# Past attention of a two-layer hybrid trunk: queries stationary in fp32, score rows turned back per four units, values fetched through a table of row numbers

## The reference, cut to what matters

```python
# layer 0, FoX, 8 heads of 64: 8 sequences x 4096 past keys, in pages of 128
k_all = concat([cache_fox_k[page_table], k]);  v_all = concat([cache_fox_v[page_table], v])
s  = einsum('bqhd,bkhd->bhqk', q, k_all) * ATTN_SCALE + cum_q - cum_k      # forgetting bias
y  = einsum('bhqk,bkhd->bqhd', softmax(where(k_idx <= pos, s, -inf)), v_all)

# layer 1, dilated, 16 heads of 64: 8 sequences x 2048 past keys, of which 1280 are within reach
for w, d in ((128, 1), (512, 4), (2048, 16)):
    idx = q_idx - d * arange(w // d + 1)          # gathered keys of one group
    m, den, o = softmax parts over k_all[idx], v_all[idx]
y  = sum(den * exp(m - max m) * o) / sum(den * exp(m - max m))
```

## Time and profile before

| | us |
|---|---|
| median of 3 runs (2656.17 to 2666.19) | 2663.16 |
| the profiled execution | 2651.5 |
| its span, first to last instruction | 2649.8 |
| PE busy | 2269.1 (86%) |
| DVE busy | 1437.8 (54%) |
| ACT busy | 872.1 (33%) |
| POOL busy | 344.8 (13%) |
| past attention of `fox`, first K transpose to last value | 244 to 616 |
| past attention of `dilated` | 1831 to 2140 |

### The profile page before, as it was taken

One profiled execution on the slowest core, in us unless ns is written; L12 is line 12 of the kernel. 1 busy time (PEld: TensorE's weight loads), 2 busy tenths in 40 slices (PEclk: granted clock), 3 DMA queues, 4 the chain that ended last, 5 costly groups with the idle time before them and its releaser, 6 DMA issues. The chain is left out here.

```text
span 2649.8 us, 64653 instructions
## 1 busy us (share of the span) xinstructions
PE 2269.1 (86%) x26373; PEld 1768.7 (67%) x26373; DVE 1437.8 (54%) x2313; ACT 872.1 (33%) x1577; POOL 344.8 (13%) x555
## 2 busy tenths in 40 slices
PE   6898888887977996889999979997867776999998
PEld 3566777776635883667777757654766655777776
DVE  2446887874563537664522265466666656453323
ACT  2335444441231212333322131155333323333222
POOL 1003233430000000101100000023111110111000
PEclk8889999998977986899999989998788788999999
DMA  7324899994274001123323324443999931332331
GB/s 249 105 84 135 317 366 381 368 387 143 85 258 120 4 3 34 48 72 91 92 80 88 88 74 141 136 151 84 274 265 287 281 94 40 89 94 80 88 88 60
DMA packets 308578, 392.58 MB, mean 148 GB/s; under 512 B 25616, under 2 KB 226650, under 8 KB 308308
## 3 DMA queue, kind: packets, MB, share of 16 engines
q1 hardware_dynamic: 276580, 282.15, 34.6%
q0 software_dynamic: 31728, 106.59, 12.4%
HBM read 377.98 MB, written 10.70 MB: 147 GB/s over the span
## 5 line engine op out<-in xcount | busy, mean ns | idle before, releaser
L820 PE MATMUL bank<-yT,WH 128*128 128x288 f16 x3200 | 533.4, 290 | 46.1 <-DVE yT L674 34.6
L820 PEld LDWEIGHTS bank<-yT,WH 128*128 128x128 f16 x3200 | 314.8, 99 | 145.2 <-issue 48.6
L884 DVE SCALAR_TENSOR_TENSOR WL<-wring,WH 128x1024 f16<-128x1024 f32 x194 | 255.3, 1320 | 259.5 <-ACT WH L864 259.4
L1367 DVE TENSOR_TENSOR KL<-bank,KH 128x512 f16<-128x512 f32 x416 | 280.6, 688 | 168.7 <-ACT KH L1347 160.4
L1347 ACT CAST KH<-bank 128x512 f16<-128x512 f32 x416 | 242.2, 584 | 353.3 <-PE bank L1265 352.1
L820 PE MATMUL bank<-uT,WH 128*128 128x288 f16 x2048 | 337.9, 288 | 10.7 <-DVE WL L884 10.7
L820 PE MATMUL bank<-yT,WL 128*128 128x288 f16 x1600 | 331.8, 290 | 0.0
L864 ACT ACTIVATE WH<-wring 128x1024 f16<-128x1024 f32 x194 | 203.5, 1054 | 268.4 <-PE bank L820 221.0
L820 PEld LDWEIGHTS bank<-uT,WH 128*128 128x128 f16 x2048 | 201.5, 98 | 63.2 <-DVE WL L884 11.3
L820 PE MATMUL bank<-uT,WL 128*128 128x288 f16 x1024 | 210.7, 288 | 0.0
L820 PE MATMUL bank<-hT,WH 128*128 128x288 f16 x960 | 162.2, 293 | 31.8 <-DVE hT L711 21.4
(11 more groups left out here) (452 smaller groups left out, 3975.2 us busy)
## 6 DMA issues: line engine op xcount, KB each, us to landing
wring<-in_ada_w SPq DMA_DIRECT2D x96, 512.0 KB, 4.5
vslot<-in_cache_fox_v POOLq DMA_DIRECT2D x182, 256.0 KB, 5.5
vTd<-in_state_dil_k SPq DMA_DIRECT2D x80, 512.0 KB, 12.8
vslot<-in_state_dil_v POOLq DMA_DIRECT2D x78, 512.0 KB, 12.7
yT<-in_cache_fox_k SPq DMA_DIRECT2D x128, 256.0 KB, 5.5
krows<-in_cache_fox_k SPq DMA_DIRECT2D x128, 256.0 KB, 5.4
wring<-in_mlp_up SPq DMA_DIRECT2D x64, 512.0 KB, 4.0
wring<-in_mlp_down SPq DMA_DIRECT2D x64, 512.0 KB, 3.9
```

The costliest lines, as they stand in the source:

```text
L820: last = nc.tensor.matmul(bank[b + h][:, 0:HALF], w[s % 2][:, c, :], x[:, s % parts * KC + c, h * HALF:(h + 1) * HALF], start=(s % parts = ...
L884: nc.vector.scalar_tensor_tensor(WL[s % 2][:, :, :], w[:, :, :], WSCALE, WH[s % 2][:, :, :], ALU.mult, ALU.subtract).then_inc(w_free, 1)
L1367: nc.vector.tensor_tensor(KL[i][:, :], turned[n % NT][:, :], KH[i][:, :], ALU.subtract).then_inc(lo_out, 1)
```

## The change

The change does the following.

1. Keys are no longer split in two f16 parts. The turned bank is copied once in fp32 (`KT`), by ACT for three units of four and by DVE for each fourth (`by_dve`: n % 4 == 1). `KH` and `KL` go. Two PSUM banks hold turned keys where there were three; the third (`backed`) takes scores turned back.
2. `products`: the queries are the weights (128x32, fp32) and the keys move (128 columns). Head pair j writes partitions 32j to 32j+31, by a tile position. Q has 32 columns a pair: 16 for an even unit and 16 for an odd one, zero elsewhere, so that an even and an odd unit add into the same 128 columns. Scores come out with queries on partitions and cached rows along the columns.
3. New steps per group of four units: ACT copies 256 columns of scores to SBUF (`take_scores`, `SQ`), PE turns them back (`turn_back`, two 128x128 fp32 transposes), DVE adds the bias in two instructions of 128 columns where there was one of 256. The DVE and softmax steps stand one slot later (`BACK = LAG + 1`), and `LEAD` goes from 2 to 3 and from 0 to 1.
4. Q: a memset of 2048 columns and 16 scalings in both layers, without the two f16 parts.
5. V of `fox` on POOL: one indirect DMA of 128 rows of 4 KB a tile, with row numbers from a table `vrow_of` in SBUF. The table is made in `load_and_turn`: a broadcast load of the page table by POOL, and four small DVE instructions between the fifth and the sixth copy of the conditioning. SP's own V loads keep the two page DMAs.
6. The loads of `lora` and `g2` (512 KB) leave POOL's list in `load_and_turn` and come at the start of `rwkv` on SP; their first reader waits for them.

The instruction order of PE in the middle of `fox` shows points 1 to 3. Before, for two units in a row: the transposes of one unit (`yT` and `krows` are K slots), then the products of the unit two before.

The diff, cut to its core:

```diff
@@ -565,8 +569,17 @@
                     copy_group(3)
                     page_rest(1)
                     copy_group(4)
+                    dve.wait_ge(pa_in, 16)
+                    nc.vector.tensor_copy(pt_f[:, :], pt_all[:, :]).then_inc(pf_ok, 1)
+                    dve.wait_ge(pf_ok, 1)
+                    nc.vector.tensor_tensor(pt_odd[:, :], pt_f[:, 1::2], pt_f[:, 0::2], ALU.subtract).then_inc(pf_ok, 1)
+                    dve.wait_ge(pf_ok, 2)
+                    nc.vector.scalar_tensor_tensor(pt_odd[:, :], pt_odd[:, :], C["place"][:, 0:1], pt_f[:, 0::2], ALU.mult, ALU.add).then_inc(pf_ok, 1)
+                    dve.wait_ge(pf_ok, 3)
+                    nc.vector.tensor_scalar(vrow_of[:, :], pt_odd[:, :], float(PAGE // 2), C["place"][:, 1:2], ALU.mult, ALU.add).then_inc(pf_ok, 1)
...
         LAG = 2
         VLAG = nu + LEAD
-        turned = [bank[i] for i in (0, 1, 6)]
+        BACK = LAG + 1
+        turned = [bank[0], bank[1]]
         scored = [bank[2], bank[3]]
+        backed = bank[6]
         mixed = [bank[5], bank[7]]
         NT = len(turned)
         with ExitStack() as sc:
...
-            KH = [sb(sc, f"KH{i}", [P, 512], F16) for i in range(NB)]
-            KL = [sb(sc, f"KL{i}", [P, 512], F16) for i in range(NB)]
+            KT = [sb(sc, f"KT{i}", [P, 512]) for i in range(NB)]
+            SQ = [sb(sc, f"SQ{i}", [P, 256]) for i in range(2)]
...
+
+            by_dve = lambda n: n % NB == 1
+
+            def wait_copied(eng, n):
+
+                if by_dve(n):
+                    eng.wait_ge(kt_d, n // NB + 1)
+                else:
+                    eng.wait_ge(kt_a, n // NB * (NB - 1) + max(n % NB, 1))
 
...
                         last.then_inc(kt_ok, 1)
 
                     def products(n):
-                        v, i, g = n // nu * E + n % E, n % NB, n // SG
-                        pe.wait_ge(lo_out, n + 1)
+                        i, g, pair, even = n % NB, n // SG, n % SG // 2, n % 2 == 0
+                        wait_copied(pe, n)
                         if n % SG == 0 and g >= 2:
-                            pe.wait_ge(sc_out, g - 1)
+                            pe.wait_ge(sq_out, g - 1)
                         for j in range(4):
-                            o = scored[g % 2][:, (n % SG) * 64 + 16 * j:(n % SG) * 64 + 16 * j + 16]
-                            jc = slice(j * P, (j + 1) * P)
-                            nc.tensor.matmul(o, KH[i][:, jc], QH[:, v, j, :], start=True, stop=False)
-                            nc.tensor.matmul(o, KH[i][:, jc], QL[:, v, j, :], start=False, stop=False)
-                            last = nc.tensor.matmul(o, KL[i][:, jc], QH[:, v, j, :], start=False, stop=True)
+                            last = nc.tensor.matmul(scored[g % 2][32 * j:32 * j + 32, pair * P:(pair + 1) * P], Q[:, n // nu * 2 + n % 2, j, :],
+                                                    KT[i][:, j * P:(j + 1) * P], start=even, stop=not even, tile_position=(0, 32 * j),
+                                                    skip_group_check=True)
                         last.then_inc(sc_ok, 1)
+
+                    def turn_back(g):
+                        pe.wait_ge(sq_out, g + 1)
+                        if g:
+                            pe.wait_ge(sc_out, 2 * g)
+                        for pair in range(2):
+                            cols = slice(pair * P, (pair + 1) * P)
+                            last = nc.tensor.transpose(backed[:, cols], SQ[g % 2][:, cols], ident)
+                        last.then_inc(bk_ok, 1)
...
+                        n = i - BACK
+                        if 0 <= n < N and n % SG == SG - 1:
+                            turn_back(n // SG)
...
                 def _(act):
-                    def high(n):
+                    def take_turned(n):
                         i = n % NB
                         act.wait_ge(kt_ok, n + 1)
                         if n >= NB:
                             act.wait_ge(sc_ok, n - NB + 1)
-                        nc.scalar.copy(KH[i][:, :], turned[n % NT][:, :]).then_inc(hi_out, 1)
+                        nc.scalar.copy(KT[i][:, :], turned[n % NT][:, :]).then_inc(kt_a, 1)
+
+                    def take_scores(g):
+                        act.wait_ge(sc_ok, (g + 1) * SG)
+                        if g >= 2:
+                            act.wait_ge(bk_ok, g - 1)
+                        nc.scalar.copy(SQ[g % 2][:, :], scored[g % 2][:, 0:256]).then_inc(sq_out, 1)
...
                 @block.vector
                 def _(dve):
-                    def low(n):
+                    def take_turned(n):
                         i = n % NB
-                        dve.wait_ge(hi_out, n + 1)
-                        nc.vector.tensor_tensor(KL[i][:, :], turned[n % NT][:, :], KH[i][:, :], ALU.subtract).then_inc(lo_out, 1)
+                        dve.wait_ge(kt_ok, n + 1)
+                        if n >= NB:
+                            dve.wait_ge(sc_ok, n - NB + 1)
+                        nc.vector.tensor_copy(KT[i][:, :], turned[n % NT][:, :]).then_inc(kt_d, 1)
 
                     def half(g):
                         s, gs = divmod(g, NG)
                         if gs == 0 and s >= 2:
                             dve.wait_ge(o_ok, s - 1)
-                        dve.wait_ge(sc_ok, (g + 1) * SG)
+                        dve.wait_ge(bk_ok, g + 1)
                         u0 = gs * SG
-                        view = lambda x: x.rearrange("p (t h q) -> p t h q", t=SG // E, q=8)
-                        nc.vector.tensor_tensor(view(ST[s % 2][:, u0:u0 + SG, :].rearrange("p t c -> p (t c)")), view(scored[g % 2][:, 0:64 * SG]),
-                                                bias_of(s, u0 // E, SG // E), ALU.add).then_inc(sc_out, 1)
+                        for b in range(2):
+                            nc.vector.tensor_tensor(ST[s % 2][:, u0 + b:u0 + SG:2, :].rearrange("p a (h q) -> p a h q", q=8),
+                                                    backed[:, 0:256].rearrange("p (a h b q) -> p a h b q", a=2, b=2, q=8)[:, :, :, b, :],
+                                                    bias_of(s, u0, b), ALU.add).then_inc(sc_out, 1)
                         if gs % 2 == 1 or gs == NG - 1:
                             p = gs // 2
-                            dve.wait_ge(sc_out, g + 1)
...
 
 
-        dst, high, rest = Q
-        zero, qb_ok = sem("zero"), sem("qb_ok")
+        zero, q_ok = sem("zero"), sem("q_ok")
 
         def on_dve(dve):
-            n = 0
-            nc.vector.memset(dst[:, :, :, :], 0.0).then_inc(zero, 1)
+            nc.vector.memset(Q[:, :, :, :], 0.0).then_inc(zero, 1)
             dve.wait_ge(zero, 1)
-            for half in range(halves):
+            for b in range(2):
                 for j in range(4):
                     for hp in range(2):
                         r = slice(64 * hp, 64 * hp + 64)
-                        n += 1
-                        nc.vector.tensor_scalar(dst[r, half::halves, j, 8 * hp:8 * hp + 8], dec(src[r, 4 * half + j, NPR:TOK]), SCALE, None,
-                                                ALU.mult).then_inc(qb_ok, 1)
-            dve.wait_ge(qb_ok, n)
-            nc.vector.tensor_copy(high[:, :, :, :], dst[:, :, :, :]).then_inc(qb_ok, 1)
-            dve.wait_ge(qb_ok, n + 1)
-            nc.vector.tensor_tensor(rest[:, :, :, :], dst[:, :, :, :], high[:, :, :, :], ALU.subtract).then_inc(qb_ok, 1)
-            dve.wait_ge(qb_ok, n + 2)
+                        at = 16 * hp + 8 * b
+                        nc.vector.tensor_scalar(Q[r, b::2, j, at:at + 8], dec(src[r, (4 * b if halves == 2 else 0) + j, NPR:TOK]), SCALE, None,
+                                                ALU.mult).then_inc(q_ok, 1)
+            dve.wait_ge(q_ok, 16)
         return on_dve
...
+            load_k, load_v_pages = load_page("cache_fox_k"), load_page("cache_fox_v")
+            v_rows = I["cache_fox_v"][0].rearrange("n (p e) h d -> (n p) (e h d)", e=2)
+
+            def load_v(eng, n, dst, done):
+
+                if eng is nc.sync:
+                    load_v_pages(eng, n, dst, done)
+                else:
+                    nc.gpsimd.indirect_dma_start(dst[:, :], None, v_rows, bass.IndirectOffsetOnAxis(ap=vrow_of[:, n:n + 1], axis=0),
+                                                 bounds_check=320 * PAGE // 2 - 1, oob_is_err=False).then_inc(done, 16)
 
             def first_reads(sp):
...
                 sp.dma_start(rc[:, :], I["cst_rwkv"]).then_inc(rc_in, 16)
+                sp.dma_start(lora[0:64, :], I["rw_w2"][0]).then_inc(lora_in, 16)
+                sp.dma_start(lora[64:128, :], I["rw_a2"][0]).then_inc(lora_in, 16)
+                sp.dma_start(g2[:, :], I["rw_g2"][0]).then_inc(lora_in, 16)
```

73 lines of the change are left out of this document (42 added, 31 removed).

## The result

The changed kernel takes 2670.76 us (median of 17 runs, 2653.53 to 2680.66), the kernel before beside it 2658.04 (17 runs): ratio 1.0038, interval 1.0022 to 1.0054. It is slower by some 10 us, within the 0.5% that was called no change. A second comparison, on the chip of the first four experiments, gave 1.0026. The forecast was 2665.5, as a sum of +2.3 us on the kernel before. The time lies 5 us from it and the sign is right, but the difference is four to six times the sum. The inside came out otherwise as well: a term that was put at nothing is +22 us, and the stage that was called bound by the transfers was not at their limit.

A forecast was written before the change was run, and what follows sets the result against it. Transfers were taken to bound `fox` and `dilated`. The terms 0 + 1.7 + 1.2 + 1.0 - 1.1 - 0.5 = +2.3 us, on the 2663.16 median, gave 2665.5 us; whole range 2645 to 2700, the forecast's own 2653 to 2677.

The forecast's parts named there:

- The steady part of `fox`, "no change": `fox` past attention, 294 to 594 us: transfers set the pace at 1.39 us a unit, 377 GB/s; change 0.
- The prediction's own sign of being wrong: Changed profile of `fox`: GB/s off 377 by over 2% would show the forecast wrong.
- TensorE's unit: Past attention: PE's unit goes from 1.06 to 1.18 us, 1.26 at the granted clock, under 1.39 in `fox`.
- the rival of 1.92 us a unit: Both pasts: 32-column products don't overlap and PE becomes the bound, 136 us in `fox`, 74 in `dilated`, 2873; chance 0.06.
- The table, "nearest: no change": V loads in `fox`: between 15 us saved and 53 lost, no change taken; POOL is not waited for in the steady part.
- The drains: Ends of the two pasts, forecast with one filling slot each: `fox` +1.7 us net, `dilated` +1.2.
- the softmax part of the step (+0.9): Drain of each past: last softmax waits for `take_scores`, `turn_back` and two more handovers, some 0.9 us each.
- the table's landings: `fox` drain: last values wait for V, table loads land later than page loads; 0 to 3.3 us, 1.5 taken.
- Small edits: Query steps 3.4 to 5.3 us in `fox`, +1.0 taken; `dilated` 1.1 less; moved `lora` and `g2` loads 0.5 less.
- The filling part: `fox`, 260 to 290 us: SP's unchanged list sets K's pace, 1.24 us a unit at 224 GB/s; one slot loses 0.3 us.
- `dilated`, "no change": `dilated` past attention: PE's unit of 1.44 us stays under the transfers' 1.88, near 279 GB/s; change 0.
- DVE and ACT: Past attention: both far from binding, ACT under 0.6 us a unit; what they are relieved of is not on the path.

The follow-up runs named there:

- the first four experiments: Changed kernel again, ratio 1.0026 to the kernel before; changed kernel with V by page, 0.9965; kernel before with the table alone, 0.9956; changed kernel in pairs of slots, 0.9928.
- the pairs with the later softmax: Pairs of slots with the table, in `fox` softmax steps three slots later and values two, against the kernel before: 2619.17 us, ratio 0.9834.
- by page: Changed kernel with V of `fox` loaded by page DMAs on POOL again, all else as changed, against the kernel before: 2650.6 us, ratio 0.9965.
- the run with five extra matmuls: Kernel before with the table and five unused fp16 matmuls of 128 columns in each unit of `fox`: 2662.35 us, ratio 1.0002.
- the old form with the table: Kernel before with V of `fox` fetched through the table and nothing else changed: 2647.01 us, ratio 0.9956.
- The pairs: Changed kernel with TensorE's list written two units at a time, halving changes of tile shape: 2640.77 us, ratio 0.9928; with V by page 2656.67 us, 1.0003.

## Why the prediction came out as it did

**The steady part of `fox`, "no change": this step failed.** It is +22 us in the changed kernel (22.6 and 22.0). The reasoning was that the transfers set the pace at 1.39 us a unit, because the DMA share was 1.00, so that 1.18 or even 1.26 of TensorE was covered. The transfers' pace is 332.9/256 = 1.30 us a unit or less, at 395 GB/s. The prediction's own sign of being wrong was a rate off 377 GB/s by over 2%; 349 is off by 7%. A share of 1.00 was no ceiling: packets of 4 KB took 170 ns in the mean before and 166 in the pairs with the later softmax, and the sixteen engines count as busy in both. The 397 of the start stood in the earlier trace rows and was used only as a bound for the table. The Trainium skill has the rule that would have asked the question ("Perfetto Trace Analysis", Roofline): a single busy core is bounded by its sixteen DMA engines at about 435 GB/s, not by its 358 share. The runs agree so far as 395 GB/s held over 300 us.

**TensorE's unit: right in kind, too small.** Forecast 1.18, measured 1.28 without waits. Transposes and products with their changes of shape were put at 0.90 and took 0.94. The turn-back was put at 0.24 for a group and took 0.37, and the values at 0.88 and took 1.00: both have a change of shape of their own, which I had given only to the products. The products did overlap, 0.36 with the changes, so the rival of 1.92 us a unit fell.

**Cover was read as all or nothing.** 1.28 against the 350.8/256 = 1.37 of the kernel before leaves 7% of room, and I treated this as full cover. Data arrive unevenly, and TensorE had been making up for each late tile by groups down to 4.35 us. With its shortest group at 5.13 us it waits 30.9 us for K with the table, and loses; by page it waits 10.4 us at the same pace, and `fox` is only 3 us over the kernel before. So the reasoning missed that the two edits meet in K's transfers. How much of the loss is TensorE's pace is open, since the run with five extra matmuls lost its time otherwise. What these runs support is a question and not a rule: how far the shortest time of the covered engine lies below the bound, and not only its mean.

**The table, "nearest: no change".** Right for its rows: 377 GB/s in the old form. Wrong in that I looked only for a price of the rows. I had written that POOL is not waited for; what it does with its time when it is faster was left out. It now waits for the values and asks for two tiles 1.3 us apart, and in the changed kernel K's tiles come later. In the old form it does the same and nothing is lost, so the strokes alone are not the cause. Asking for the second tile some 0.3 us later took 9 us of the 19 back; the rest stays open.

**The drains.** Forecast +1.7 and +1.2. `fox` was 2.4 shorter, and 2.1 shorter in the old form with the table, 0.9 longer with pages alone. So the softmax part of the step (+0.9) would fit, while the table's landings, for which I took 1.5 us from the two loads of the start, cost nothing: the table gives back 2 to 3 us there. In `dilated`, from the last key transpose to the end of the stage, TensorE took 17.7 us for 18.1, so the +0.9 does not show.

**Small edits.** The query steps were as worked out:

```profile
141.87 1.76 DVE L1506 MEMSET Q<- 128x2048 f32 x1 [0.38 <-DVE qkT L921]
143.66 3.50 DVE L1513 TENSOR_SCALAR Q<-qkT 64x64 f32<-64x64 f32 x16
147.20 1.23 DVE L897 SCALAR_TENSOR_TENSOR WL<-wring,WH 128x1024 f16<-128x1024 f32 x1
```

That is 5.3 us for 3.4. Their part in the time can't be seen: the first K transpose came at 242.3 to 248.2 us in the ten executions with them and at 244.0 to 246.9 in the four without. The filling part moved 214 GB/s for 224, as steady as was forecast.

**`dilated`, "no change".** This held: 1.28 against 1.88 is room enough, and 289.4 to 300.2 is no different from the old form's 292.6 to 295.6. The pairs took it to 275.4 to 278.1 in three of four executions, so TensorE's pace had a part in it all the same.

**DVE and ACT.** That their relief (241 to 139 us of DVE in 300) would bring nothing was right for the changed kernel. It was half the truth: the order of VectorE's list costs TensorE time at each start of a sequence, in the kernel before as well, and I had read no waits by place in the sequence.

That the whole came near 2665.5 is luck. The kernel before is 2658.04 us in 17 runs, 5 us below the three that the forecast stood on, and the medians differ by 12.7 us for the 2.3 of the sum. Against the 22 us of `fox` stand two things that were not forecast: the shorter drain, and time elsewhere. Ten executions with the table took 1197.9 to 1211.5 between the pasts, four with pages 1209.8 to 1214.2, with nearly the same instructions; the granted clock falls at another point of that part. Whether the table causes this or chance does stays open. That the old form with the table is 12 us below the kernel before in its median, with 1.5 more in its `fox`, speaks against chance alone.

## What to carry to other kernels

A DMA share of 1.00 says that the engines are occupied, not that they can't move more; look for the best stretch of the trace and ask why the others don't reach it. Before an engine is called covered, compare the bound with its shortest period and look at its waits by place in the loop, because a stall of 4 us once in eight groups is lost in a mean. A faster issuer that ends up waiting for slots turns even requests into strokes; here that cost 19 us in one form of the kernel and nothing in the other, so two edits that are harmless alone have to be tried together. A load that is put on an engine to imitate a slower one also adds to its own time: it needs a control, and its waits have to be read.

## What the runs showed of the hardware

- A change between full-width and 32-column tiles costs 0.10 to 0.14 us each way: four transposes to the next product took 0.48 us in the earlier trace rows and 0.58 here, 32 value matmuls to what follows 0.88 and 1.00. Halving the changes of units took the shortest group from 5.13 to 4.56 us, 0.14 for each of four changes.
- The same stage moved 377 GB/s at a DMA share of 1.00 and 395 at 1.01, one core alone.
- An indirect load of 128 rows of 4 KB takes GpSimd 1.3 us of its list, the two page loads that it replaces 2.3; on SyncE a page load takes 1.24.
- The granted clock of the same part of the program, some 330 to 430 us behind the end of `fox`, fell at different points from execution to execution and moved its length by up to 16 us: more than most of the edits here are worth.
